# Two norm stages of a small transformer stack: the sum of one quarter cut in two, and four low halves placed ahead of the last sum

## What is computed

```
def rms_norm_2(x, g):
    y = xf * lax.rsqrt(jnp.mean(xf * xf, axis=-1, keepdims=True) + RMS_EPS)
    return (y * g).astype(x.dtype)
...
    for i in range(DEPTH):
        h = h + 0.5 * rms_norm_2(swiglu(rms_norm_2(h, g[0]), ffn_w13[i, 0], ffn_w2[i, 0]), g[1])
        hn = rms_norm_2(h, g[2])
        m = gmlp_mixer(hn, ...) if i % 2 == 0 else rwkv7_mixer(hn, ...)
        h = h + rms_norm_2(m, g[3])
        h = h + 0.5 * rms_norm_2(swiglu(rms_norm_2(h, g[4]), ffn_w13[i, 1], ffn_w2[i, 1]), g[5])
        gate = jax.nn.sigmoid(rms_norm_2(h, g[6]) @ ple_w_gate[i])
        h = h + rms_norm_2(gate * (p[i] @ ple_w_proj[i]), g[7])
```

## Time and profile before

| | |
|---|---|
| time, median of 3 executions | 2162.55 us (2160.2 to 2165.48) |
| profiled execution, span from first to last instruction | 2163.4 us |
| instructions | 39049 |
| PE busy | 2125.5 us, 98% |
| DVE busy | 1520.1 us, 70% |
| ACT busy | 1151.6 us, 53% |
| POOL busy | 366.7 us, 17% |
| mean granted TensorE clock | 0.998 |

### The profile page before, as it was taken

The page is one execution under the profiler, slowest core; times in us unless marked ns, Lnnn a source line. Parts: engine busy times, 40 slices in busy tenths (PEclk is TensorE's granted clock), DMA queues, the critical chain, the costliest instruction groups (busy, mean ns, idle before and its releaser), DMA issues.

```text
span 2163.4 us, 39049 instructions
## 1 busy us (share of the span) xinstructions
PE 2125.5 (98%) x13574; PEld 1806.7 (84%) x13574; DVE 1520.1 (70%) x2382; ACT 1151.6 (53%) x1983; POOL 366.7 (17%) x462
## 2 busy tenths in 40 slices
PE   8999999999999999999999999999999999899998
PEld 7888788888888788888888988888888777778887
DVE  6666976667667966677667757667766777767666
ACT  5445754545547655455455445446644554445445
POOL 1111211112111211122110002111111112301111
PEclk9999999999999999999999999999999999999999
DMA  7655445555555345546556545556555441026553
GB/s 252 203 181 185 138 134 198 183 194 183 186 196 190 108 155 195 192 167 204 191 187 234 174 157 194 181 197 233 175 197 182 163 147 61 13 108 196 198 181 129
DMA packets 104110, 375.53 MB, mean 174 GB/s; under 512 B 11696, under 2 KB 12208, under 8 KB 104016
## 3 DMA queue, kind: packets, MB, share of 16 engines
q1 hardware_dynamic: 104016, 374.24, 51.3%
HBM read 373.15 MB, written 1.05 MB: 173 GB/s over the span
## 4 chain that ended last, share of the span: by engine, by line
PE 85%; DVE 7%; ACT 4%; issue 2%; POOL 1%; DMA 1%; SPq 0%; DVEq 0%; POOLq 0%; ACTq 0%
PE bank L938 27%; PE bank L942 14%; PE bank L187 13%; PE bank L188 12%; PE bank L189 12%; DVE w_lo L181 2%; ACT act L477 1%; DMA work<-pt_dram 1%; PE bank L1221 1%; ACT w_hi L174 1%; DVE act L587 1%; PE bank L2206 0%; PE bank L387 0%; DVE x L572 0%; ACT work L439 0%
## 5 line engine op out<-in xcount | busy, mean ns | idle before, releaser
L938 PE MATMUL bank<-act,w_hi 128*128 128x512 f32 x2816 | 704.4, 392 | 3.8 <-DVE work L883 2.2
L938 PEld LDWEIGHTS bank<-act,w_hi 128*128 128x128 f32 x2816 | 514.8, 188 | 107.5 <-DVE act L587 4.2
L798 DVE TENSOR_TENSOR w_lo<-raw,w_hi 128x1024 fp32r<-128x1024 f32 x432 | 502.9, 1220 | 4.3 <-issue 1.0
L789 ACT ACTIVATE w_hi<-raw 128x1024 fp32r<-128x1024 f32 x432 | 424.9, 1050 | 2.3
L942 PEld LDWEIGHTS bank<-act,w_lo 128*128 128x128 f32 x2816 | 384.1, 190 | 27.6
L942 PE MATMUL bank<-act,w_lo 128*128 128x256 f32 x2816 | 392.5, 282 | 0.0
L889 DVE TENSOR_TENSOR work<-bank,work 128x256 f32<-128x256 f32 x176 | 74.8, 425 | 376.8 <-ACT work L819 376.8
L181 DVE TENSOR_TENSOR w_lo<-raw,w_hi 128x1024 fp32r<-128x1024 f32 x248 | 294.8, 1220 | 56.8 <-ACT w_hi L174 56.6
L850 POOL TENSOR_TENSOR work<-work,rb 128x256 f32<-128x256 f32 x176 | 129.6, 737 | 1038.0 <-DVE work L883 1038.0
L187 PE MATMUL bank<-w_hi,g_hi 128*128 128x512 f32 x704 | 277.0, 393 | 0.9 <-DVE w_lo L181 0.3
L188 PE MATMUL bank<-w_lo,g_hi 128*128 128x512 f32 x704 | 275.9, 392 | 0.0
(11 more groups left out here) (288 smaller groups left out, 2251.3 us busy)
## 6 DMA issues: line engine op xcount, KB each, us to landing
raw<-w_dram SPq DMA_DIRECT2D x680, 512.0 KB, 4.4
work<-rows_dram SPq DMA_DIRECT2D x13, 512.0 KB, 6.7
work<-rrows_dram SPq DMA_DIRECT2D x5, 512.0 KB, 3.7
x<-x_dram SPq DMA_DIRECT2D x2, 512.0 KB, 3.9
out<-x SPq DMA_DIRECT2D x4, 256.0 KB, 2.0
work<-g_dram SPq DMA_DIRECT2D x1, 640.0 KB, 9.9
work<-dist_dram SPq DMA_DIRECT2D x2, 256.0 KB, 4.8
work<-ws_dram SPq DMA_DIRECT2D x1, 512.0 KB, 8.3
```

Of the source, the lines that this page charges most:

```text
L789: nc.scalar.activation(c.w_hi[:, n % RING, :], c.raw[:, n % RING, :], ACT.Copy).then_inc(c.hi_ready, 1)
L798: nc.vector.tensor_tensor(c.w_lo[:, n % RING, :], c.raw[:, n % RING, :], c.w_hi[:, n % RING, :].bitcast(F32), ALU.subtract).then_inc(c.lo_ ...
L938: nc.tensor.matmul(bank[:, :], c.w_hi[:, slot(m), k * P:(k + 1) * P], c.act[:, k, :, :], start=k == 0, stop=False)
```

## The change

In joins A to D (`self.cut`):
- the sum of quarter (1,0), the second in the order of the sums and the third in the order of rows, is made in two pieces of 256 columns, so `x_new` counts 5 instead of 4. PE turns tiles 0 and 1 behind the first piece and tiles 2 and 3 behind the second, each with its own count of `turned`;
- ACT's high half 0 waits for the first two turned tiles only, and high half 2 for the next two. Its square of quarter (1,0) waits for the second piece;
- DVE makes the low halves 0 to 3 behind the third sum, and the last sum, of quarter (1,1), behind low half 3;
- the tiles lie in other banks: `PLACE_CUT`.

In the two joins of order `ROWS` (A and the `plain` one) the mean of token tile 1 (`mean_y(dve, 3)`) is moved ahead of the gains of quarters (1,0) and (1,1). In the gated projection at the end of layer 0, the gain of quarter (0,1) is moved behind the product of quarter (1,1) and the mean of token tile 0, and the gain of (1,1) behind the mean of token tile 1.

The diff, cut to its core:

```diff
@@ -304,6 +304,7 @@
...
+    PLACE_CUT = [5, 7, 0, 1, 2, 3, 2, 3]
...
+        self.cut = row is not None and plain is None and not units_first
...
+        elif self.cut and self.turned == 2:
+            pe.wait_ge(s["x_new"].sem, s["x_new"].at(2))
+            self.turn_tiles(pe, t, range(0, 2))
+            pe.wait_ge(s["x_new"].sem, s["x_new"].at(3))
+            self.turn_tiles(pe, t, range(2, 4))
+            return
         else:
-            pe.wait_ge(s["x_new"].sem, s["x_new"].at(self.turned))
-        for k in range(4 * h, 4 * h + 4):
-            last = self.nc.tensor.transpose(self.tile(k)[:, t * P:(t + 1) * P], c.x[:, t, k * P:(k + 1) * P], c.ident)
-        last.then_inc(s["turned"].sem, 1)
+            pe.wait_ge(s["x_new"].sem, s["x_new"].at(self.pieces(self.turned)))
+        self.turn_tiles(pe, t, range(4 * h, 4 * h + 4))
...
+    def pieces(self, quarters):
+
+        return quarters + (1 if self.cut and quarters >= 2 else 0)
...
@@ -435,7 +451,7 @@
...
-            act.wait_ge(s["x_new"].sem, s["x_new"].at(i + 1))
+            act.wait_ge(s["x_new"].sem, s["x_new"].at(self.pieces(i + 1)))
...
-        if k % 4 == 0:
+        if self.cut and k in (0, 2):
             act.wait_ge(s["turned"].sem, s["turned"].at(2 + k // 2))
+        elif k % 4 == 0:
+            act.wait_ge(s["turned"].sem, s["turned"].at(self.pieces(2 + k // 2)))
...
-        self.nc.vector.scalar_tensor_tensor(self.x(t, h), y, by, self.x(t, h), ALU.mult,
-                                            ALU.add).then_inc(s["x_new"].sem, 1)
+        x = self.x(t, h)
+        for part in (slice(0, S), slice(S, HALF)) if self.cut and (t, h) == (1, 0) else (slice(0, HALF),):
+            self.nc.vector.scalar_tensor_tensor(x[:, part], y[:, part], by, x[:, part], ALU.mult,
+                                                ALU.add).then_inc(s["x_new"].sem, 1)
...
-            if self.order[i][1] == 1:
+            rows = self.waiting and self.order is self.ROWS
+            if self.order[i][1] == 1 and not (rows and i == 3):
                 self.mean_y(dve, i)
             self.gain_y(dve)
             if self.waiting and self.order[i] == (0, 1):
                 self.add_y(dve)
+                if rows:
+                    dve.wait_ge(s["y_squares"].sem, s["y_squares"].at(4))
+                    self.mean_y(dve, 3)
+        if self.cut:
+            while self.added < 3:
+                self.add_y(dve)
+            while self.made_low < 4:
+                self.low(dve)
...
@@ -2852,9 +2881,15 @@
                 if last and h == 1 and t == 0:
                     out.first_token(dve)
                     continue
-                if h == 1 and t == 1 and not last:
-                    out.mean_y(dve, 2)
+                if h == 1 and not last:
+                    continue
                 out.gain_y(dve)
+        if not last:
+            out.mean_y(dve, 2)
+            out.gain_y(dve)
+            out.mean_y(dve, 3)
+            out.gain_y(dve)
+            return
         out.mean_y(dve, 3)
```

More of the change, by code:

```diff
@@ L323, in __init__ @@
             self.gain, self.gain_number = c.next_gain()
-        counts = {"turned": 4, "low": KT, "root": 2}
+        counts = {"turned": 5 if self.cut else 4, "low": KT, "root": 2}
         if plain is None:
@@ L327, in __init__ @@
         if not start:
-            counts |= {"quad": quads, "x_new": 4}
+            counts |= {"quad": quads, "x_new": 5 if self.cut else 4}
         if row is not None or post is not None:
@@ L355, in tile @@
         at = (k // 2 % 2) * S
-        return self.c.bank[self.PLACE[k]][:, at:at + S]
+        return self.c.bank[(self.PLACE_CUT if self.cut else self.PLACE)[k]][:, at:at + S]
     def gain_of(self, k):
@@ L383, in turn, with turn_tiles @@
             pe.wait_ge(c.x_in[t].sem, c.x_in[t].at(16))
-        else:
-            pe.wait_ge(s["x_new"].sem, s["x_new"].at(self.turned))
-        for k in range(4 * h, 4 * h + 4):
-            last = self.nc.tensor.transpose(self.tile(k)[:, t * P:(t + 1) * P], c.x[:, t, k * P:(k + 1) * P], c.ident)
-        last.then_inc(s["turned"].sem, 1)
+        elif self.cut and self.turned == 2:
[4 more added lines that the diff above has]
+            return
+        else:
+            pe.wait_ge(s["x_new"].sem, s["x_new"].at(self.pieces(self.turned)))
+        self.turn_tiles(pe, t, range(4 * h, 4 * h + 4))
+    def pieces(self, quarters):
+        return quarters + (1 if self.cut and quarters >= 2 else 0)
+    def turn_tiles(self, pe, t, tiles):
+        for k in tiles:
+            last = self.nc.tensor.transpose(self.tile(k)[:, t * P:(t + 1) * P],
+                                            self.c.x[:, t, k * P:(k + 1) * P], self.c.ident)
+        last.then_inc(self.s["turned"].sem, 1)
     def tensor(self, pe):
@@ L660, in __init__ @@
     def __init__(self, c, by, sources, row, out):
-        self.order, self.adds, self.early = self.QUADS, self.ROWS, False
+        self.order, self.adds, self.early, self.cut = self.QUADS, self.ROWS, False, False
         self.y_squared = self.y_gained = self.added = 0
```

## The result

The changed kernel takes 2175.66 us in the median of 4 executions (2173.26 to 2177.55), the kernel before 2161.73 (2160.2 to 2165.48, 4 executions): 13.9 us more, ratio 1.0065 with a 95% interval of 1.0053 to 1.0077. In a later series it took 2173.86 against 2160.26: 1.0057, 1.0043 to 1.0071. It is slower, and by some 4 to 5 us more than the 9.3 forecast. The median still lies inside the stated range of 2167 to 2176, 0.3 under its upper end.

What follows compares the result with a forecast made beforehand. PE, busy 98% of the span, was taken to bound the kernel, so late first products count whole: 2.1 + 2.3 + 2.7 + 2.3 - 0.1 = +9.3 us, a median of 2171.8 us, range 2167 to 2176.

Steps and rivals of the forecast that it cites:

- What bounds, and that nothing catches up a late start: PE, busy 98% of the span, has no slack behind joins; a late first product goes whole into the end.
- The core, the last turns behind four low halves: In joins A to D PE's first product waits for low halves 0 to 3, last sum and turns; B 2.63 us late.
- Four terms: Net lateness of the four cut joins: A +2.1, B +2.3, C +2.7, D +2.3 us.
- The mean: In the plain join, the mean moved ahead of the gains starts the sums 0.1 us earlier: -0.1 us.
- Projection's order: In join C the gain of (1,1) behind the mean of token tile 1 makes the sums start 0.34 us late.
- the clock: Rival, 10%: PE's clock falls in the new join gaps, 3.4 us a join; 2175 to 2179 for one or two, 2185 for all.
- a PEclk under 1.00 in a join: Sign that the forecast is wrong; it expected a granted clock of 1.00 in all four joins.
- The argument for zero: Against the clock falling in joins: turns stand on both sides of the gap, and the 1 us gaps didn't do it.
- The price of a fall: A fallen clock under full products behind a join was put at 3.4 us a join, 13.6 in all four.
- The base: The profiled span before, 2163.4 us, was taken as 0.9 above the runs' median of 2162.55.
- Absorbed: Rival, 8%: DVE and ACT set the pace behind joins, so only their slip counts: +4.1 us, 2166.7.
- Not slower because the low halves are a head start: Rival, 4%: the first product needn't wait for the last turns; each join -0.3 to +0.2 us, whole 2162 to 2163.

Runs made afterwards that it cites:

- 10: The changed kernel with five filler products in PE's queue ahead of the last turns in each gap: 2171.92 us against 2160.26 before, ratio 1.0052.
- 9: The changed kernel as it is, measured again in a later series: 2173.86 us against 2160.26 before, ratio 1.0057.
- experiment 4: The changed kernel with the last four turns put behind PE's first products: 2166.2 us against 2160.77 before, ratio 1.0020.
- experiment 7: The kernel before without its filler products ahead of the turns in five joins: 2165.72 us against 2160.64 before, ratio 1.0021.
- the filler runs: The changed kernel with five filler products in each of PE's gaps, run in two series: 2174.74 us (ratio 1.0060) and 2171.92 us (ratio 1.0052).
- 8: The changed kernel with the last sum before low half 0, old projection order, high halves ahead of later squares in B, C, D: 2161.8 us, ratio 1.0004.
- 11: The kernel before with token tile 1's mean ahead of the gains in ROWS joins, high halves ahead of later squares in B, C, D: 2160.97 us, ratio 0.9999.

## Why the prediction came out as it did

**What bounds, and that nothing catches up a late start: right but for 0.2 us in A.** In the stretches behind A, B and C PE waited for nothing but 0.2 us for a weight unit in each of the last two, and C to the plain join shows join C's lateness whole, +2.50. In A 0.2 of the late start was given back, where I had read from a busy time of 139.50 in 139.50 that there was nothing to give: PE's products overlap, so a start that is late by some hundredths doesn't show as idle time.

**The core, the last turns behind four low halves: right.** Four terms against what the profile shows (first products, less what is given back): A 2.1 and 1.75; B 2.3 and 2.2; C 2.7 and 2.5; D 2.3 and 2.2 (its first product comes 2.45 later, 7.90 behind the last one against 5.45, less the 0.2 of stall ahead of tiles 4 to 7). The mean: -0.1 and -0.14. Sum 9.3 and 8.5, and the profiled execution of 10 has 9.1. The single times were right to 0.1: a piece is 0.40 apart from the next; the square of (1,0) starts 0.90 behind the first piece, forecast 0.91; the last sum 2.37 behind high half 0, forecast 2.34. Two of them made the sum too high by 0.09 a join each: the first product came 0.47 behind the last sum's end where I had 0.56, and high half 0 came 0.63 behind the start of its square where I had 0.71. The 0.2 given back in A comes on top.

**Projection's order: right.** Join C's sums start at 1518.77:

```profile
1517.22 0.16 DVE L575 SCALAR_TENSOR_TENSOR small<-small 128x1 f32<-128x1 f32 x1
...
1518.09 0.16 DVE L575 SCALAR_TENSOR_TENSOR small<-small 128x1 f32<-128x1 f32 x1
...
1518.77 2.20 DVE L592 SCALAR_TENSOR_TENSOR x<-work,small,x 128x512 f32<-128x512 f32 x4
```

That is 1.55 behind the mean of token tile 0, where it was 1.25 (1512.71 to 1513.96): 0.30, forecast 0.34.

**Where the size was off: the clock, a term that the forecast put at zero.** The median rose 13.9 and 13.6, not 9.3. The clock had 10% as a rival, and it fell in A and D in the first profile of the change, in A, B and C in that of 9, and with the low halves alone in all four joins. By the forecast's own sign, a PEclk under 1.00 in a join, it was wrong here. The argument for zero, that turns stand on both sides and gaps of 1 us hadn't done it, was too weak: gaps of 2.46 did it, once one of 0.80 (experiment 4), and in experiment 7 idle gaps of 0.83 to 3.51 without any late work in A and B cost 5.1 us. The profile of the change adds up: 8.5 of lateness and 3.1 of clock are 11.6, and its execution took 2173.26, 11.5 above 2161.73. The other three took 2175.17 to 2177.55 at mean clocks of 0.994 to 0.996 against its 0.998, so the clock fell for longer in them; where, no profile shows. That the whole 4 to 5 us are the clock's is argued from this and from the mean clocks; the medians of the filler runs don't settle it.

The price of a fall was put too high: 3.4 us forecast, 2.5 and 2.6 measured for the longer falls of 9, 1.4 to 1.6 for the shorter ones. The rival had 2175 to 2179 for one or two falls; 2175.66 lies at its lower end with two falls in the profile, and 2173.86 under it with three. So it is partly luck that the median lies in the range: the late products were put 0.8 too high, and the range's upper end had room for one fall.

The warning that I had put beside the rival (the Trainium skill, TensorE: Matmul & The Clock Gate, "HAM oscillation — how this bites in real kernels": idle gaps take TensorE back to the half clock, and the work behind starts slow) bore on this case, but I had stretched it: the page's rule is for longer gaps than 2.46 us, and by it alone these joins would not have been hit. Here the measurement decides: behind gaps of 2.46 us a product started 0.43 behind the last one instead of 0.23.

**The base.** That the profiled execution before was an average one was wrong: it held a fall of the clock in the recurrence, 3 us, that nine of the twelve other profiles don't have. It shifted the difference of the two profiles down to 8.1 and hid the clock's share; the forecast's difference, 9.3 on the median, wasn't touched.

**The other rivals fell.** Absorbed (8%): no, the lateness arrived in full (+2.50 for C). Not slower because the low halves are a head start (4%): the program's order held the first product behind the last turns; experiment 4 shows that the head start exists once the turns are moved, and that it is used up by the later halves and the weight units behind them.

## What to carry to other kernels

Before moving work ahead on one engine, look at what the next engine's queue has in front of the work that is to profit: four low halves made early are worth nothing while PE's queue first wants the last turns. Follow what is pushed back, too: in experiments 4, 8 and 11 the weight units behind the low halves came late, and PE waited for them 9 to 12 us behind its first product. Price a new gap on PE twice, once for its length and once for the clock behind it, and read the granted clock in windows around the gap. And read the mean clock of every execution, since a profile is only one of them.

## What the runs showed of the hardware

Lateness and clock are separable: in both profiles with fillers that fit the gap the clock was 1.00 in every join, at unchanged distances (A 7.74 and 7.73, B 12.99 and 12.96). A fall in a join cost 1.4 to 1.6 us of PE's time where it was short, 2.5 to 2.6 where it was long. A filler of 128x256 in float32 is two matmuls, 0.45 us together at the upper level (ten in 2.32). Whether a join is hit depends on more than its gap: with the same gap of 2.46, B and C were spared and D hit in the first profile of the change, and B and C hit and D spared in that of 9. What decides it stays open.
